# Input projection of a fp32 hybrid mixer layer: unit pairs as seven block products in place of eight

## The reference, cut to what matters

```
hm = rmsnorm(x, norm_g) * (1 + scale) + shift
proj = hm @ w_in                                    # w_in: 1024 x 6144
u_a, z_a, b_b, c_b, v_b, z_b = split(proj, 6)
y_a = real(fftn(u_a in groups of 256)) * silu(z_a)
y_b = b_b * dwconv3(c_b * v_b, conv_w) * silu(z_b)
x = x + gate * (concat(y_a, y_b) @ w_out)
```

## Time and profile before

| | |
|---|---|
| median of three runs | 1177.57 us (1176.67 to 1178.69) |
| the profiled execution | 1178.75 us, its span 1176.9 us |
| busy: PE, PE's weight loads | 1113.4 us (95%), 1040.3 us |
| busy: DVE, ACT, POOL | 747.5, 508.8, 255.0 us |
| the first layer's units from unit 3 on | 63.5 to 424 us |
| the output projection after them | 425 to 507 us and a tail |

### The profile page before, as it was taken

How to read it: one execution, slowest core, us unless ns; L and a number is a source line. 1 busy time by engine, 2 the same in 40 slices (tenths; PEclk the granted TensorE clock), 3 DMA queues, 4 the chain that set the end, 5 groups by cost and what they waited for, 6 DMA issues and landing times.

```text
span 1176.9 us, 19282 instructions
## 1 busy us (share of the span) xinstructions
PE 1113.4 (95%) x7195; PEld 1040.3 (88%) x7195; DVE 747.5 (64%) x1277; ACT 508.8 (43%) x1024; POOL 255.0 (22%) x383
## 2 busy tenths in 40 slices
PE   5899999999999999999899999999999999879997
PEld 3799999999999988888899999999999999867785
DVE  1655434767575433647869696969696978766444
ACT  5322222121212133335565666666656666565321
POOL 1200000000000000012033443444443444443001
PEclk8899999999999999999999999999999999989999
DMA  9753122344444252214325343434343424272702
GB/s 314 247 154 108 53 89 89 108 136 152 150 136 143 72 203 84 84 36 161 82 92 137 87 134 104 130 108 130 108 125 100 129 83 132 81 261 92 287 19 90
DMA packets 177880, 148.06 MB, mean 126 GB/s; under 512 B 7004, under 2 KB 156868, under 8 KB 177428
## 3 DMA queue, kind: packets, MB, share of 16 engines
q1 hardware_dynamic: 172772, 130.08, 35.9%
q0 software_dynamic: 4608, 16.83, 4.3%
q10 hardware_dynamic: 432, 0.21, 0.1%
HBM read 134.32 MB, written 12.78 MB: 125 GB/s over the span
## 4 chain that ended last, share of the span: by engine, by line
PE 65%; DVE 14%; ACT 11%; issue 5%; DMA 3%; POOL 2%; SPq 0%; DVEq 0%; ACTq 0%; POOLq 0%
PE PS L295 27%; PE PS L491 15%; PE PS L1372 9%; DVE big L1582 3%; DVE big L1559 3%; PE PS L1358 2%; ACT big L1493 2%; ACT big L1505 2%; PE PS L1431 2%; ACT w_hi L262 1%; PE PS L741 1%; DMA big<-y_scr 1%; DMA big<-l_scr 1%; PE PS L1133 1%; DVE w_lo L268 1%
## 5 line engine op out<-in xcount | busy, mean ns | idle before, releaser
L268 DVE TENSOR_TENSOR w_lo<-raw_w,w_hi 128x1024 fp32r<-128x1024 f32 x128 | 162.2, 1269 | 87.7 <-ACT w_hi L262 86.1
L262 ACT ACTIVATE w_hi<-raw_w 128x1024 fp32r<-128x1024 f32 x128 | 134.4, 1052 | 109.8 <-PE PS L295 72.2
L295 PE MATMUL PS<-h_hi,w_hi 128*128 128x320 f32 x720 | 164.8, 310 | 0.0
L295 PE MATMUL PS<-h_lo,w_hi 128*128 128x320 f32 x720 | 164.1, 309 | 0.0
L295 PE MATMUL PS<-h_hi,w_lo 128*128 128x320 f32 x720 | 164.0, 309 | 0.0
L295 PEld LDWEIGHTS PS<-h_hi,w_hi 128*128 128x128 f32 x720 | 120.0, 188 | 3.4 <-ACT big L950 2.5
L295 PEld LDWEIGHTS PS<-h_hi,w_lo 128*128 128x128 f32 x720 | 120.4, 188 | 0.0
L295 PEld LDWEIGHTS PS<-h_lo,w_hi 128*128 128x128 f32 x720 | 120.3, 188 | 0.0
L1358 PE MATMUL PS<-h_hi,w_hi 128*128 128x320 f32 x480 | 118.2, 327 | 0.0
L1358 PE MATMUL PS<-h_hi,w_lo 128*128 128x320 f32 x480 | 109.4, 309 | 0.0
L1358 PE MATMUL PS<-h_lo,w_hi 128*128 128x320 f32 x480 | 109.2, 309 | 0.0
(11 more groups left out here) (234 smaller groups left out, 2299.1 us busy)
## 6 DMA issues: line engine op xcount, KB each, us to landing
raw_w<-in_fc_w_in_dram SPq DMA_DIRECT2D x48, 512.0 KB, 4.4
raw_w<-in_ssd_w_in_dram SPq DMA_DIRECT2D x48, 512.0 KB, 5.0
big<-l_scr SPq DMA_DIRECT2D x40, 512.0 KB, 4.5
...
big<-in_w_mod_dram SPq DMA_DIRECT2D x16, 512.0 KB, 8.2
raw_w<-in_fc_w_out_dram SPq DMA_DIRECT2D x16, 512.0 KB, 3.6
raw_w<-in_ssd_w_out_dram SPq DMA_DIRECT2D x16, 512.0 KB, 8.1
...
```

The lines of the kernel that those rows point to most:

```text
L262: act.activation(w_hi[:, slot, :], raw_w[:, slot, :], ACT.Copy).then_inc(hi_ready, 1)
L268: dve.tensor_tensor(w_lo[:, slot, :], raw_w[:, slot, :], w_hi[:, slot, :].bitcast(F32), ALU.subtract).then_inc(lo_ready, 1)
L295: mm = pe.matmul(PS[:, 2 * pair + s, 0:HALF], w[:, slot, ws], h[:, kt, s * HALF:(s + 1) * HALF], start=(kt == 0 and n == 0), stop=(kt == K ...
```

## The change

Units 0 to 3 stay. Units 4 to 47 become 22 pairs (n = 2 to 23, in the same order of channels). A pair is a product of 2 x 2 blocks: output channels in two blocks of 128, k in two halves of 512, tokens in two halves of 320. It is made of seven block products (`part_pe`, B11, T2, B21, T3, T1, T4, B22), each four k-tiles of three matmuls of 320 columns into one PSUM bank, 84 matmuls for 96.

- Weights: a pair comes in four quarters of 128 x 512, 256 KB each (`quarter_loads`). POOL makes four sums of quarters (`weights_pool`), and the seven operands are split into high and low by ACT and DVE, 512 columns each (`part_hi`, `part_lo`), a pair ahead.
- Tokens: four sums of token blocks are made and split once, before pair 2 (DVE `fourier_first_dve`, four sums and four low parts of 1280 columns; ACT four high parts).
- Results: ACT copies the first product out of PSUM (320 columns), DVE makes seven combinations of 320 columns, one operand in PSUM, the other in SBUF (`combined` counts them). PE waits for them before it uses a bank again. The gate's SiLU is then applied in SBUF, c is no longer copied by ACT, and c x v and b x conv have both operands in SBUF.
- The centre tap moves from DVE to ACT; the product with the conv gate from DVE to POOL (`yb_pool`).
- The modulation tiles are loaded one at a time (32 DMAs of 512 KB on POOL's queue) and placed by a table: 22 within the pairs, 10 in the output projection, with the last two of the four reduces.
- No hardware loops are left in the layer's projection: all groups are written out.

The diff, cut to its core; the old functions of the same stage are removed.

```diff
-N_IN0 = 48
+N_PLAIN = 4
+PAIRS = range(2, 24)
+PARTS = 7
...
+        B11, T2, B21, T3, T1, T4, B22 = range(PARTS)
+        BANK = (0, 1, 2, 3, 0, 1, 2)
+        U2, C11, U3, C22, TS, C21, C12 = range(1, 8)
...
+        def token_part(r, kt):
+            if r == B11:
+                return h_hi[:, kt, H0], h_lo[:, kt, H0]
+            if r == B21:
+                return h_hi[:, 4 + kt, H0], h_lo[:, 4 + kt, H0]
+            if r == T4:
+                return h_hi[:, 4 + kt, H1], h_lo[:, 4 + kt, H1]
+            hi, lo = {T2: S2, T3: S3, T1: S1, B22: S4}[r]
+            return hi[:, kt, :], lo[:, kt, :]
+        def part_pe(pe, n, r):
+            pe.wait_ge(lo_ready, pair_base(n) + r + 1)
+            for kt in range(4):
+                ws = slice(kt * P, (kt + 1) * P)
+                hh, hl = token_part(r, kt)
+                for j, (w, h) in enumerate(((qhi[r], hh), (qhi[r], hl), (qlo[r], hh))):
+                    mm = pe.matmul(PS[:, BANK[r], 0:HALF], w[:, ws], h, start=(kt == 0 and j == 0), stop=(kt == 3 and j == 2))
+            mm.then_inc(unit_used, 3 if (n, r) == (23, B22) else 1)
+        def pair_pe(pe, n):
+            if n == 7:
+                mod_reduce_pe(pe, 0, 4)
+            if n == 15:
+                mod_reduce_pe(pe, 1, 4)
+            if n == 2:
+                pe.wait_ge(act_freed, 4)
+            else:
+                pe.wait_ge(combined, sums(n - 1, TS))
+            part_pe(pe, n, B11)
+            if n == 2:
+                pe.wait_ge(s_done, 5)
+            else:
+                pe.wait_ge(combined, sums(n - 1, C21))
+            part_pe(pe, n, T2)
+            if n > 2:
+                pe.wait_ge(combined, sums(n - 1, C12))
+            part_pe(pe, n, B21)
+            if n == 2:
+                pe.wait_ge(s_done, 6)
+            part_pe(pe, n, T3)
+            if n == 2:
+                pe.wait_ge(s_done, 7)
+            pe.wait_ge(p1_copied, n - 1)
+            part_pe(pe, n, T1)
+            pe.wait_ge(combined, sums(n, U2))
+            part_pe(pe, n, T4)
+            pe.wait_ge(combined, sums(n, C11))
+            if n == 2:
+                pe.wait_ge(s_done, 8)
+            part_pe(pe, n, B22)
...
+        def part_hi(act, n, r):
+            if n == 2:
+                act.wait_ge(unit_used, r // 2 + 1)
+            else:
+                act.wait_ge(unit_used, pair_base(n - 1) + r + 1)
+            if r in (B11, B21, B22):
+                quarter_wait(act, n, {B11: 0, B21: 1, B22: 3}[r])
+            else:
+                act.wait_ge(w_sums, 4 * (n - 2) + {T1: 1, T2: 2, T4: 3, T3: 4}[r])
+            act.activation(qhi[r], b22_raw[n % 2] if r == B22 else qraw[r], ACT.Copy).then_inc(hi_ready, 3 if (n, r) == (23, B22) else 1)
+        def part_lo(dve, n, r):
+            dve.wait_ge(hi_ready, pair_base(n) + r + 1)
+            dve.tensor_tensor(qlo[r], b22_raw[n % 2] if r == B22 else qraw[r], qhi[r].bitcast(F32), ALU.subtract).then_inc(
+                lo_ready, 3 if (n, r) == (23, B22) else 1)
+        def weights_pool(pool, n):
+            quarter_wait(pool, n, 0)
+            if n == 2:
+                pool.wait_ge(lo_ready, 3)
+            else:
+                pool.wait_ge(lo_ready, pair_base(n - 1) + T1 + 1)
+            pool.tensor_tensor(qraw[T1], qraw[T3], qraw[B11], ALU.subtract).then_inc(w_sums, 1)
+            quarter_wait(pool, n, 1)
+            pool.wait_ge(w_sums, 4 * n - 7)
+            pool.tensor_tensor(qraw[T2], b22_raw[n % 2], qraw[T1], ALU.subtract).then_inc(w_sums, 1)
+            if n > 2:
+                pool.wait_ge(lo_ready, pair_base(n - 1) + T4 + 1)
+            pool.wait_ge(w_sums, 4 * n - 6)
+            pool.tensor_tensor(qraw[T4], qraw[T2], qraw[B21], ALU.subtract).then_inc(w_sums, 1)
+            pool.tensor_tensor(qraw[T3], b22_raw[n % 2], qraw[T3], ALU.subtract).then_inc(w_sums, 1)
...
+        MOD_TILE = {2: 0, 3: 2, 5: 5, 7: 8, 8: 11, 9: 12, 11: 13, 12: 14, 13: 15, 15: 16, 16: 17, 17: 18, 19: 19, 20: 20, 21: 21}
+        def pair_dve(dve, n):
+            base, i, k = pair_base(n), turn(n), kind(n)
+            dst = pair_dst(n)
+            if n in (4, 6, 8):
+                ya_dve(dve, n // 2 - 1)
+            if n < 23:
+                part_lo(dve, n + 1, B11)
+            dve.wait_ge(unit_used, base + T2 + 1)
+            dve.wait_ge(p1_copied, n - 1)
+            if n > 2:
+                dve.wait_ge(combined, sums(n - 1, C12))
+            dve.tensor_tensor(u2, PS[:, BANK[T2], 0:HALF], s1, ALU.add).then_inc(combined, 1)
+            if k == "b":
+                tap_left(dve, i, 0)
+            dve.wait_ge(unit_used, base + B21 + 1)
...
+            dve.tensor_tensor(dst[:, 0, H0], PS[:, BANK[B21], 0:HALF], s1, ALU.add).then_inc(combined, 1)
+            if k == "b":
+                tap_right(dve, i, 0)
+            if n in MOD_TILE and k not in ("v", "c"):
+                mod_tile_dve(dve, MOD_TILE[n])
+            dve.wait_ge(unit_used, base + T3 + 1)
+            dve.wait_ge(combined, sums(n, U2))
+            dve.tensor_tensor(u3, u2, PS[:, BANK[T3], 0:HALF], ALU.add).then_inc(combined, 1)
+            if n < 23:
+                part_lo(dve, n + 1, T2)
...
+            dve.wait_ge(unit_used, base + T1 + 1)
+            dve.wait_ge(combined, sums(n, U3))
+            dve.tensor_tensor(dst[:, 1, H1], PS[:, BANK[T1], 0:HALF], u3, ALU.add).then_inc(combined, 1)
+            dve.tensor_tensor(u2, PS[:, BANK[T1], 0:HALF], u2, ALU.add).then_inc(combined, 1)
+            if n < 23:
+                part_lo(dve, n + 1, B21)
...
+            if k == "b":
+                tap_left(dve, i, 1)
+            dve.wait_ge(unit_used, base + T4 + 1)
+            dve.tensor_tensor(dst[:, 0, H1], u3, PS[:, BANK[T4], 0:HALF], ALU.subtract).then_inc(combined, 1)
...
+            if n < 23:
+                part_lo(dve, n + 1, T3)
+                part_lo(dve, n + 1, T1)
...
+            dve.wait_ge(unit_used, base + B22 + 1)
+            dve.wait_ge(combined, sums(n, TS))
+            dve.tensor_tensor(dst[:, 1, H0], PS[:, BANK[B22], 0:HALF], u2, ALU.add).then_inc(combined, 1)
...
+            if k == "v":
+                dve.wait_ge(combined, sums(n, C12))
+                dve.tensor_tensor(cv[:, 1, :], cv[:, 1, :], cv_c[:, 1, :], ALU.mult).then_inc(conv_mult, 1)
+            if k == "b":
+                tap_right(dve, i, 1)
+                dve.wait_ge(combined, sums(n, C12))
+                dve.wait_ge(conv_step, ctaps[0])
+                dve.tensor_tensor(cc[:, 1, :], cv_c[:, 1, :], cc[:, 1, :], ALU.mult).then_inc(conv_mult, 2)
+            if k == "za":
+                ab_dve_ops(dve, i)
+            if n < 23:
+                part_lo(dve, n + 1, T4)
+                part_lo(dve, n + 1, B22)
...
+            if n == 2:
+                mod_tile_dve(dve, 1)
+            if k == "za":
+                mod_tile_dve(dve, MOD_TILE[n] + 1)
+                mod_tile_dve(dve, MOD_TILE[n] + 2)
...
+            if n in MOD_TILE and k in ("v", "c"):
+                mod_tile_dve(dve, MOD_TILE[n])
...
+        def yb_pool(pool, i):
+            for j in range(2):
+                pool.wait_ge(conv_mult, 6 * i + (4, 6)[j])
+                pool.wait_ge(gates_done, 6 + 2 * i + j + 1)
+                pool.tensor_tensor(yT[:, 8 + 2 * i + j, :], cc[:, j, :], sz_b[:, j, :], ALU.mult).then_inc(yb_done, 1)
...
+        def quarter_loads(sp, n):
+            pair = PAIR_COLS[n]
+            for q, (slot, kt0, col) in enumerate(((0, 0, pair[0]), (2, 4, pair[0]), (3, 0, pair[1]), (6, 4, pair[1]))):
+                if n == 2:
+                    sp.wait_ge(lo_ready, slot // 2 + 1)
+                elif q < 3:
+                    sp.wait_ge(lo_ready, pair_base(n - 1) + slot + 1)
+                elif n == 3:
+                    sp.wait_ge(lo_ready, 4)
+                else:
+                    sp.wait_ge(lo_ready, pair_base(n - 2) + slot + 1)
+                if q != 2 and n > (3 if q == 3 else 2):
+                    sp.wait_ge(w_sums, 4 * (n - 4) + 4 if q == 3 else 4 * (n - 3) + (1, 3)[q])
+                sp.dma_start((b22_raw[n % 2] if q == 3 else qraw[slot]).rearrange("p (k n) -> p k n", n=P),
+                             fc_src[:, kt0:kt0 + 4, col:col + P]).then_inc(half_landed[q % 2], 16)
...
+            fourier_first_pe(pe)
+            for n in PAIRS:
+                pair_pe(pe, n)
+                if n < 8 and n % 2:
+                    dft_pe(pe, n // 2)
```

More of the change, by code:

```diff
@@ L467, in out_act @@
             for n, q in list(enumerate(SPLITS[layer]))[first:]:
+                if layer == 0 and q == 8:
+                    mod_row_act(act, 2)
                 y_split_act(act, layer, q)
@@ L767, in start_pe, with kind, turn, pair_cols @@
                 unit_part_pe(pe, u, kts)
-        def fourier_pe(pe, i, first):
-            for k in range(3 if first else 0, 4):
-                pe.wait_ge(lo_ready, 4 * i + k + 1)
-                pe.wait_ge(act_freed, 4 * i + k - 1)
-                channel_tile(pe, k, k % 2)
+        def kind(n):
```

(56 more changed lines are left out.)

578 lines of the change are left out of this document (323 added, 255 removed).

## The result

The changed kernel takes **1191.93 us** (median of 4 runs, 1190.13 to 1193.33) against 1177.93 for the kernel before on the same chip: ratio 1.012, 95% interval 1.0107 to 1.0132. The forecast was 1168.0 and "faster" had 0.74. It is slower, and lies above the range.

The account below looks back on a forecast made before the run. PE bounds the projection before; after, DVE with POOL's lock bounds the conv pairs. Terms -38.7 + 3 x 7.5 + 2.4 + 2.7 + 1.0 + 0.5 = -9.6 give 1169.2, less 1.2: 1168 us, range 1145 to 1184.

Parts of the forecast that it names:

- The lock: POOL's sums and DVE's operations with two SBUF operands take turns; a 512 column sum holds DVE 0.96 us.
- PE, 22 pairs: In the first layer's projection, 84 matmuls a pair instead of 96, 12.31 us, 1.76 less each: 38.7 us off.
- conv turns over 4 x 49.2: Turns of four pairs: DVE's list plus lock, 56.7 us, 7.5 over PE's 49.2 three times; last 51.6, 2.4 over.
- Fourier groups over 3 x 33.9: Groups of two pairs and a transform: DVE 34.8 us with lock against PE's 33.9, 0.9 over, three times 2.7.
- start: Before the pairs, new token sums and splits on DVE, copies on ACT, mostly covered by PE: 1.0 us, bounds 0 and 6.
- output projection: Ten modulation tiles, 24.8 us of DVE, move into its 82 us and mostly fit: 0.5 us, bounds 0 and 5.
- loops written out: Projection loops unrolled: costed at nothing, since PE had no idle time at their ends to win.
- DVE's own list: DVE's work in a conv turn without the lock: 44.9 us, fitting under PE's 49.2 by itself.
- The wait per sum: DVE waits two thirds of a hold, 0.64 us, for each of 16 sums a turn, plus 1.6 for two products.
- DVE pays every hold: Rival: DVE waits a full 0.96 a sum, turn 62.6, time 1198; decides from about 0.78 on; chance 0.15.
- ACT and the loads: In the pairs, ACT's 5 us of 12.3 a pair and weight quarters, asked for a pair later, cost nothing.
- The granted clock: Sign of being wrong: TensorE's granted clock falling below full in the gaps.

Follow-up runs that it names:

- experiment 1: Changed kernel with POOL's four weight sums of a pair cut to 1 column of 512, waits kept: 1147.16 us, 0.9737 of before.
- experiment 6: One-column DVE memsets added in the output projection: changed kernel with 40, 1185.34 us, with 80, 1185.19; kernel before with 56, 1185.02, with 24, 1185.06.
- Experiment 4: Changed kernel with eight extra unused matmuls of 320 columns ahead of part B11 from pair 10 on: 1192.64 us, 1.0114 of before.
- experiments 5 and 2: Changed kernel: 5, splits of pairs 10 to 23 read one operand from PSUM, 1173.28 us; 2, POOL's sums replaced by memsets that only write, 1148.92 us.

## Why the prediction was wrong

The lock was right, in kind and nearly in size. What failed is that DVE was given no idle time while it is the bound; and one loss was not in the prediction at all. By its terms, in us:

| term | forecast | measured |
|---|---|---|
| PE, 22 pairs | -38.7 | -38.7 |
| conv turns over 4 x 49.2 | +24.9 | +34.5 |
| Fourier groups over 3 x 33.9 | +2.7 | +10.8 |
| start | +1.0 | -0.7 |
| output projection | +0.5 | +1.0 |
| second layer ("loops written out", costed at nothing) | 0 | +6.6 |
| sum | -9.6 | +13.5 |

(The reduces of 1.2 us that lie in a turn and in a group are taken off; two more moved from the pairs to the output projection, 2.4 us, and cancel. The spans differ by 12.9.)

- **PE.** Right. A pair takes 12.31 us where nothing stops it.
- **DVE's own list.** 44.9 us a turn forecast; 42.8 busy with the sums away (experiment 1), of which the two products hold 0.7. Right that by itself it fits, but put some 3 us too long.
- **The wait per sum.** Forecast 0.64 us for each of 16 sums and 0.8 for each of two products. These are the groups of the third turn, in the changed kernel and in experiment 1:

```profile
L911 DVE TENSOR_TENSOR w_lo<-raw_w,w_hi 128x512 fp32r<-128x512 f32 x29 | 28.2, 996 | 2.9 <-ACT w_hi L906 2.9
L1271 DVE SCALAR_TENSOR_TENSOR big<-big,cond 128x1024 f32<-128x1024 f32 x6 | 10.8, 1832 | 0.0
```

```profile
L911 DVE TENSOR_TENSOR w_lo<-raw_w,w_hi 128x512 fp32r<-128x512 f32 x28 | 19.1, 709 | 2.0 <-ACT w_hi L906 2.0
L1271 DVE SCALAR_TENSOR_TENSOR big<-big,cond 128x1024 f32<-128x1024 f32 x6 | 7.4, 1277 | 0.0
```

  Taken operation by operation, each against its length where it isn't held, DVE's work of this turn is 11.1 us longer beside the 16 sums, **0.69** each, and 2.7 beside the two products, 1.3 each. In all four turns it is 0.69 a sum as well, in the Fourier groups 0.76. With the hold of 1.09 (experiment 1) the share is 0.63, so "two thirds" was right. The 0.96 was near by some luck: the earlier trace rows were reduced by columns alone (0.67 and 1.07), while the prediction's own price from start to start is 1.14 for 1024 columns; by that the hold is 0.41 and its double 0.82. The rival "DVE pays every hold" named the outcome, slower, but needs 0.78 a sum for it, and that isn't what was measured.
- **DVE's turn taken as its list plus the lock is the step that failed.** DVE's busy time came out as forecast: 219.6 us in the four turns against 3 x 56.7 + 51.6 = 221.7, 106.3 in the Fourier groups against 3 x 34.8 = 104.4. That the sum agrees so well is luck, since the list was too long and the lock too small. But the seven stretches last 346.3 us, and in **20.3** of them DVE is idle, where the prediction had none. 11.5 us go to ACT's high parts, 3.4 to ACT's copies in the transforms, 2.7 to PE. Less the two reduces, which PE does meanwhile, that is 17.9 us, and by 17.7 the turns and groups were missed.
- **ACT and the loads, "costed at nothing", are most of it.** Three of the four turns have one wait of 2.2 us at the same place, the first split in DVE's list of the turn. Here DVE waits for ACT, and ACT for the load of the quarter, which can only be issued once an earlier split has freed its slot:

```profile
315.25 1.16 DVE L911 TENSOR_TENSOR w_lo<-raw_w,w_hi 128x512 fp32r<-128x512 f32 x1 [2.16 <-ACT w_hi L906]
```

```profile
314.58 0.63 ACT L906 ACTIVATE w_hi<-raw_w 128x512 fp32r<-128x512 f32 x1 [1.53 <-DMA raw_w<-in_fc_w_in_dram]
```

  The prediction reckoned when PE asks for a part ("some 15 us after", "a pair later"), but DVE works its list in order and stands at the split long before. A second wait of 0.7 to 0.9 us in each turn is for ACT behind POOL's second sum. In the third turn 56.8 busy and 3.6 idle are the 60.4. This is read from the trace; no run takes these waits away and leaves the sums.
- **Fourier groups.** Forecast at 0.9 over PE each. Without the sums they take 36.3, 33.4 and 34.6 us, 1.4 over PE in all three once the reduce is taken off; with them 41.1, 36.2 and 36.4. DVE's busy time there was forecast at 34.8 a group and is 36.8, 34.8 and 34.7; the rest is again its idle time, 1.1 of it in each group for ACT's copy out of the transform.
- **Start, output projection.** Both near; ten tiles there take 1.277 us an operation, alone.
- **Costed at nothing: the loops written out.** The prediction looked only for idle time at the loops' ends, and not at what a longer stream does to a loop behind it. 6.6 us, shown by experiment 6 from both sides. Without it the forecast would still have missed: the kernel would stand at 1185.3, still slower.
- **The granted clock** was named as a sign of being wrong, and it fell four times in the pairs. Experiment 4 and DVE's short waits for PE show that next to nothing of the time hangs on it there. In the second layer it falls behind each stall (from 736.9 and 863.2) and its price is inside the 6.6 us.
- **The rule.** The Trainium skill, page "SBUF — State Buffer", section "Who interferes with whom", calls the port pair that the two engines share an exclusive lock, and says, of DVE's two-port modes, that whoever comes first has it for the whole instruction. By that the forecast had 0.83 us a sum, a turn of 60 and 1184 us. The trace lies between: a hold of 1.09 us where the prediction had 0.96 and an estimate of 1.24 for the whole operation; the shortest of the 88 sums took 1.26 us. The turn of 60 came about in another way, by idle time. The section also says that a DVE instruction with at most one SBUF input, outside those modes, and a GpSimd one that only writes don't contend; experiments 5 and 2 agree (0.681 us, and 0.722 for 0.695).
